# Two of the seven low halves of a chunk's inputs are taken from one step of the down projection into the next

## The reference

```
def conv_glu(h, row_len, w_up, ffn_conv_w, w_down):
    u, gt = jnp.split(h @ w_up, 2, axis=-1)
    gt = grid_conv3x3(gt, ffn_conv_w, row_len)
    return (jax.nn.gelu(gt) * u) @ w_down
...
    x = x + gate2 * conv_glu(h, row_len, w_up, ffn_conv_w, w_down)
```

## Time and profile before

| | us |
|---|---|
| median of 3 runs | 1531.93 |
| lowest and highest | 1529.87, 1535.61 |
| the profiled execution, time | 1531.26 |
| its span in the trace | 1529.4 |
| mean granted TensorE clock | 0.985 |

### The profile page before, as it was taken

One profiled execution on the slowest core, in us unless ns is written; L12 is line 12 of the kernel. 1 busy time (PEld: TensorE's weight loads), 2 busy tenths in 40 slices (PEclk: granted clock), 3 DMA queues, 4 the chain that ended last, 5 costly groups with the idle time before them and its releaser, 6 DMA issues. The chain is left out here.

```text
span 1529.4 us, 26363 instructions
## 1 busy us (share of the span) xinstructions
PE 1440.4 (94%) x10534; PEld 1393.4 (91%) x10534; DVE 1100.3 (72%) x1613; ACT 597.5 (39%) x1110; POOL 743.5 (49%) x495
## 2 busy tenths in 40 slices
PE   4999999999999999996859999999999999999997
PEld 2888999999998998995859899999999989999996
DVE  4651463569996896327989766776676699999967
ACT  5322254221157785214423333333333343322324
POOL 0011111560133453223677667677666677877840
PEclk9999999999999999999979999999999999999999
DMA  9835124532416468221102121212212164333103
GB/s 336 290 138 200 62 79 130 170 114 87 144 67 191 124 194 326 88 88 36 51 16 71 66 80 71 83 63 82 76 60 87 71 240 168 107 132 134 59 29 124
DMA packets 92109, 181.04 MB, mean 118 GB/s; under 512 B 20172, under 2 KB 53524, under 8 KB 89684
## 3 DMA queue, kind: packets, MB, share of 16 engines
q1 hardware_dynamic: 88100, 169.72, 32.3%
q10 hardware_dynamic: 3456, 7.87, 1.3%
q0 software_dynamic: 432, 1.77, 0.3%
HBM read 140.99 MB, written 38.35 MB: 117 GB/s over the span
## 5 line engine op out<-in xcount | busy, mean ns | idle before, releaser
L2938 PE MATMUL ps<-hH,wH 128*128 128x384 f32 x696 | 237.9, 342 | 0.5 <-DVE hL L2257 0.5
L2940 PE MATMUL ps<-hL,wH 128*128 128x384 f32 x696 | 233.1, 335 | 0.0
L1627 POOL TENSOR_TENSOR wL<-sumQ,wH 128x512 fp32r<-128x512 f32 x120 | 167.5, 1398 | 121.0 <-ACT wH L2090 120.7
L2667 DVE SCALAR_TENSOR_TENSOR ps<-G,cst,ps 128x1024 f32<-128x1024 f32 x168 | 216.5, 1289 | 5.0
L1544 POOL TENSOR_TENSOR wL<-raw,wH 128x1024 fp32r<-128x1024 f32 x32 | 80.2, 2508 | 257.2 <-ACT wH L1838 256.7
L1627 POOL TENSOR_TENSOR wL<-raw,wH 128x512 fp32r<-128x512 f32 x90 | 124.0, 1381 | 76.4 <-ACT wH L2090 76.4
L2938 PE MATMUL ps<-hH,wL 128*128 128x384 f32 x696 | 158.1, 334 | 0.0
L2090 ACT ACTIVATE wH<-sumQ 128x512 fp32r<-128x512 f32 x120 | 75.6, 631 | 206.5 <-PE ps L3194 135.6
L2938 PEld LDWEIGHTS ps<-hH,wH 128*128 128x128 f32 x696 | 131.1, 188 | 8.4 <-issue 6.7
L3194 PE MATMUL ps<-hH,wH 128*128 128x288 f32 x480 | 136.0, 297 | 1.9 <-DVE fa L2697 1.9
L3197 PE MATMUL ps<-hL,wH 128*128 128x288 f32 x480 | 135.0, 295 | 0.0
(11 more groups left out here) (453 smaller groups left out, 4155.4 us busy)
## 6 DMA issues: line engine op xcount, KB each, us to landing
raw<-wts SPq DMA_DIRECT2D x103, 512.0 KB, 4.2
araw<-wts SPq DMA_DIRECT2D x48, 512.0 KB, 6.1
p_d<-fa SPq DMA_DIRECT2D x22, 576.0 KB
X<-xT SPq DMA_DIRECT2D x8, 1152.0 KB, 12.3
kv<-tok_d SPq DMA_DIRECT2D x16, 512.0 KB, 5.3
fs0B<-p_d SPq DMA_DIRECT2D x9, 576.0 KB, 6.6
tok_d<-stage ACTq DMA_DIRECT2D x18, 256.0 KB, 2.0
gb<-grow_d SPq DMA_DIRECT2D x18, 256.0 KB, 4.0
```

The lines of the kernel that those rows point to most:

```text
L1627: gp.tensor_tensor(grouped(m, ring(wL, i)), form_source(m, j), grouped(m, ring(wH, i)).bitcast(F32), ALU.subtract).then_inc(s["wl_ready"], 1)
L2667: last = V.scalar_tensor_tensor(dst, src, w(3 * dy + dx), dst, ALU.mult, ALU.add)
L2938: last = M(out, lhs, rh[:, c], start=(k == 0 and not lo), stop=(lo and k == kts - 1))
L2940: M(out, lhs, rl[:, c], start=False, stop=False)
```

## The change

```diff
@@ -2809,11 +2809,13 @@
                         add(m, p, q)
                     if m == UP_STEPS and p in (P1, P5, P6, P3):
                         part_low(0, {P1: "B22", P5: "T3", P6: "B21", P3: "T4"}[p])
+                    if m > UP_STEPS and m % 2 == 0 and p in (P1, P5):
+                        part_low(c - 1, {P1: "B21", P5: "T4"}[p])
                     if c < GROUPS:
                         if m % 2 == 0 and p in (P3, P7, P2, P4):
                             part_sum(c, {P3: "T1", P7: "T2", P2: "T3", P4: "T4"}[p])
-                        if m % 2:
-                            part_low(c, PARTS[p])
+                        if m % 2 and p in (P1, P5, P6, P7, P2):
+                            part_low(c, {P1: "B11", P5: "T1", P6: "T2", P7: "B22", P2: "T3"}[p])
```

## The result

| | before | changed |
|---|---|---|
| median, us (20 runs each) | 1531.97 | 1522.77 |
| lowest and highest | 1523.37, 1539.70 | 1515.09, 1537.21 |
| ratio of the times | 1 | 0.9949 [0.9925, 0.9972] |
| the profiled execution | 1531.26 | 1521.37 |
| its span | 1529.4 | 1519.5 |

The forecast was 1524.9 us in a range from 1521.8 to 1530.2. The medians lie 9.2 us apart where 7.0 were forecast, and the interval of the ratio reaches from 4.3 to 11.5 us. Both kernels were timed again beside the later experiments, and gave 0.9964 [0.9942, 0.9987], or 6.0 us. So the change is worth 0.4 to 0.5%, and the runs of one kernel scatter by two to three times as much (16 and 22 us from lowest to highest).

The account below looks back on a forecast made before the run. TensorE bounds the whole span, but in steps 22 to 27 it waits for VectorE's late adds, losing 8.6 us; 1.6 remain, so 1531.93 - 7.0 = 1524.9 us, range 1521.8 to 1530.2.

Parts of the forecast that it names:

- What can be saved, 8.6 us: PE's waits for DVE's adds, P6 of step 22 to P6 of step 28: 8.35 us, plus 0.25 at the start.
- What is saved, 7.0 us: Over steps 22 to 28, 1.6 of 8.6 us of PE's waits remain, so 7.0 us are saved.
- B22, from 2.3 to 1.3 us: Odd step, behind P7: B22's low half falls into POOL's idle 2.30 us and takes 1.3 us, where it took 2.3.
- the walk: DVE's order followed from P3's adds of step 23: four moved halves cost 7.0 us if T4's is free, 8.5 before.
- T3, 2.3 us: Odd step, behind P2: T3's low half falls into POOL's chain of sums and takes 2.3 us, where it took 1.6.
- B21, 2.1 us: Even step, behind P1: B21's low half meets POOL and takes 2.1 us, where it took 2.3.
- T4, 1.3 or 2.3 us: Even step, behind P5: T4's low half slips between two POOL instructions (1.3 us) or waits for one (2.3).
- What remains, 1.6 us: PE's loss left after the change: 0.37 us in step 23 and 0.6 each in steps 25 and 27.
- The sign: If the forecast is right, DVE has no idle time at P3 of steps 24 and 26.
- Rival 1: Steps 22 to 27: DVE is full, its 46.1 us a chunk do not shrink; 4.4 us saved, 1527.5; chance 0.2.
- Rival 2: Even steps: moved subtractions delay POOL's weights' low parts and PE waits for them; no gain, 1531 us; chance 0.1.
- rival 3: Each chunk's wait gathers in one place, PE's clock falls; slower, 1538 to 1544 us; chance 0.05.

Follow-up runs that it names:

- second pair of profiles: Kernel before and changed kernel, both unchanged, traced and timed again; ratio of changed to before 0.9964 [0.9942, 0.9987].

## Why the prediction was right, step by step

- **What can be saved, 8.6 us.** Right but for 0.1 us (0.16 and not 0.25 at P6 of step 22). With contention taken away the old order ran at full pace (Z 132.7), and so did the change with T2 moved.
- **What is saved, 7.0 us.** 7.6 in Z and 0.16 at P6 of step 22; in the second pair of profiles 5.7, because one chunk of that run of before was itself shorter.
- **How it is saved.** Here the number was better than the account. The forecast lets DVE's work fall by 1.5 us a chunk, 4.5 in Z, and gets the other 2.3 us or so from a better use of DVE's time, since it lets no idle time stand. Measured are 7.3 us from less work and 0.3 from less idle time. Two errors of opposite sign all but cancelled, which is luck. Some of the idle time is forced, as PE's 44.2 us a chunk are more than the 43.6 that DVE now works; but with 44.9 us of work, in the run that moves B21 and T4 alone, 0.9 us a chunk stayed idle as well.
- **B22, from 2.3 to 1.3 us.** Right: 1.34 as a row, inside POOL's idle time. The waits before P4, P1 and P5 went as the walk said.
- **T3, 2.3 us.** Wrong, 1.34. This is the term of the sum that was mis-sized. I let DVE be the one that waits, as the half falls into POOL's chain of sums; the sum's row begins 0.07 us before DVE's, and the sum waited instead. That took 1 us more than forecast off DVE's work in every chunk.
- **B21, 2.1 us.** 2.47 to 2.49 in three of four steps, 1.35 in the fourth. **T4, 1.3 or 2.3 us:** 1.34 in three, 2.16 in the fourth. The walk named this chance of a lower price, and it is the half of the saving that the move into the even step gives. Both lie on the ends of my bound, and when one is dear the other is cheap, so their sum was about right: 3.5 to 3.8 us as rows, which is 3.35 to 3.65 from start to start, against 3.4 to 4.4 forecast.
- **What remains, 1.6 us.** 0.9 by the three waits before P2. They exceed the 0.8 us of Z because blocks took 1.56 us from P4 of step 23 to P7 of step 25. The 0.25 us a chunk that I let DVE carry over was not there: with T3 cheap, a chunk asks 43.6 us of DVE, less than PE's 44.2, and its idle time at P1 of each even step (0.74 to 0.76 us) shows that lateness is back at nothing. The sign that I had named for it, no idle time at P3 of steps 24 and 26, missed at step 24 by 0.16 us.
- **Rival 1** (DVE is full whatever the order, mean of 1.9 us a subtraction) fell in its number: the 28 low halves of chunks 1 to 4 have a mean of 1.72 us where they had 2.02, and the 21 within Z 1.74 for 2.09, which is 2.4 us less a chunk. Its other half held, that every microsecond of DVE's work counts. The chunk was as long as DVE's busy time and 0.8 to 1.2 us of idleness in every chunk in which PE had to wait, from 43.4 us of work to 46.2. **Rival 2** (waits for `wL`) and **rival 3** (the clock) showed nowhere in steps 22 to 28; the clock was 1.00 in all of them.
- **The chances.** The measured 0.5% is just on the bound between faster and the same, as the sum said, and either was given about even odds. Scatter was larger than I took it to be: a few us between runs were 22 between the extremes.

## What to carry over

An engine that is below its limit over the whole span can bind another in one stage. Sum its work per chunk there, and see how late it may be before someone waits (3.2 us by this forecast's sum). Where VectorE's instructions with two inputs in SBUF run beside GpSimd, their place is also their price: of the 7.6 us saved here, 7.3 are VectorE's own time, given back by three instructions (B22, T3 and T4) that met GpSimd less. So when an edit moves work on such an engine, measure its busy time before and after, over the same instructions, before crediting the new order with the gain. And where whole times scatter by more than an edit is worth, judge it by a stretch between two named instructions, in two runs of each kernel.

## What the runs showed beyond that

- **Matmuls at three paces under one granted clock.** Blocks of 12 take 1.58 us in most stretches, 1.61 through steps 22 to 27 of one run and through a chunk of each of two others, and 1.56 in some (P4 of step 23 to P7 of step 25 of the changed kernel), at 1.00 in all. Most changes of pace stand right behind a block that was held up. What sets the pace was not tried and is open. At 1.61 the subtractions met GpSimd otherwise: B22 and T3 took 1.34 us in their old places (2.37 and 1.72 at 1.58), and the loss all but disappeared. So what an order costs depends on PE's pace.
- **Who waits when VectorE and GpSimd meet is decided by little.** T3's half and POOL's sum stand 0.07 us apart and POOL waits, though its row begins first; before, with 0.49 us left of POOL's low part, DVE's half took 1.71. The dear one of B21 and T4 changes between steps of one run.
- **Scatter on one core.** Whole times of one program lie up to 22 us apart, and the first block of step 20 begins anywhere between 1241 and 1258 us. So most of it arises ahead of the down projection; in the stretch from 0 to 200 us the granted clock was 0.96 in some profiles and 0.98 in others. Whether that is the cause was not tried.
